# Up-projections of three feed-forward parts as three fp32r products

## What is computed

```python
def swiglu(h, w1, w3, w2):
    return (jax.nn.silu(h @ w1) * (h @ w3)) @ w2
...
def conv_ffn(h, w_up, conv_w, conv_b, w_down):
    val, gate = jnp.split(h @ w_up, 2, axis=-1)
    gate = lax.conv_general_dilated(gate, conv_w.astype(gate.dtype), window_strides=(1,),
...
    return (jax.nn.silu(gate) * val) @ w_down
```

## Time and profile before

| | before |
|---|---|
| median of three runs | 2951.45 us (2946.42 to 2951.50) |
| the profiled execution | 2939.45 us |
| its span in the trace | 2937.4 us |
| TensorE busy | 2642.8 us (90%) |
| VectorE busy | 963.7 us (33%) |
| ScalarE busy | 580.1 us (20%) |
| TensorE's mean granted clock | 0.963 of 2.4 GHz |

### The profile page before, as it was taken

One profiled execution on the slowest core, in us unless ns is written; L12 is line 12 of the kernel. 1 busy time (PEld: TensorE's weight loads), 2 busy tenths in 40 slices (PEclk: granted clock), 3 DMA queues, 4 the chain that ended last, 5 costly groups with the idle time before them and its releaser, 6 DMA issues.

```text
span 2937.4 us, 37122 instructions
## 1 busy us (share of the span) xinstructions
PE 2642.8 (90%) x15307; PEld 1697.0 (58%) x15307; DVE 963.7 (33%) x1571; ACT 580.1 (20%) x913; POOL 213.0 (7%) x256
## 2 busy tenths in 40 slices
PE   5998999999778878879999999989989998788998
PEld 2764758744433434436767767765447855554883
DVE  2304420011401001005646656640123115992111
ACT  2111610001100000004545535510001111001110
POOL 1401200000000000000000000000000032550000
PEclk8998999999899999999999999989999999888999
DMA  8527164456899999998757747754537444504441
GB/s 298 101 100 242 23 206 150 153 187 259 335 395 392 395 395 393 394 394 295 258 169 264 258 172 254 248 184 145 205 133 233 157 153 149 229 1 149 146 157 57
DMA packets 287695, 648.51 MB, mean 221 GB/s; under 512 B 12498, under 2 KB 102765, under 8 KB 274176
## 3 DMA queue, kind: packets, MB, share of 16 engines
q10 hardware_dynamic: 151440, 358.68, 33.5%
q1 hardware_dynamic: 129744, 272.83, 26.6%
q0 software_dynamic: 6368, 14.96, 2.5%
HBM read 645.38 MB, written 1.05 MB: 220 GB/s over the span
## 4 chain that ended last, share of the span: by engine, by line
PE 71%; DMA 13%; DVE 7%; ACTq 4%; issue 3%; ACT 1%; POOL 0%; DVEq 0%; POOLq 0%
PE bank L1368 21%; PE bank L1384 12%; DMA ring<-in_moe_w 11%; PE bank L591 5%; PE bank L593 4%; PE bank L592 4%; PE bank L1635 4%; ACTq L459 3%; PE bank L606 3%; DVE H L1996 2%; PE bank L603 1%; PE bank L1723 1%; DVE arena L1203 1%; PE bank L565 1%; PE bank L1526 1%
## 5 line engine op out<-in xcount | busy, mean ns | idle before, releaser
L1368 PE MATMUL bank<-HT,ring 128*128 128x256 f32 x2816 | 616.4, 382 | 5.4 <-issue 2.7
L1368 PEld LDWEIGHTS bank<-HT,ring 128*128 128x128 f32 x2816 | 538.8, 192 | 83.4 <-issue 4.6
L944 DVE TENSOR_TENSOR w_low<-ring,w_high 128x1024 fp32r<-128x1024 f32 x252 | 305.3, 1224 | 127.9 <-ACT w_high L749 125.7
L1384 PE MATMUL bank<-ring,arena 128*128 128x512 f32 x784 | 340.7, 596 | 0.7 <-ACT arena L1104 0.7
L749 ACT ACTIVATE w_high<-ring 128x1024 fp32r<-128x1024 f32 x252 | 265.3, 1059 | 195.6 <-PE bank L593 194.0
L1384 PEld LDWEIGHTS bank<-ring,arena 128*128 128x128 f32 x784 | 149.6, 191 | 188.8 <-issue 187.5
L565 PE MATMUL bank<-ring,arena 128*64 128x256 f32 x1120 | 135.8, 385 | 43.7 <-DMA ring<-in_moe_w 43.6
L526 PE MATMUL bank<-ring,arena 128*64 128x256 f32 x1120 | 134.9, 384 | 44.2 <-DMA ring<-in_moe_w 44.2
L928 DVE TENSOR_TENSOR HT<-HT,bank 128x256 f32<-128x256 f32 x35 | 14.7, 421 | 442.7 <-PE bank L565 425.6
L591 PE MATMUL bank<-w_high,tokens_low 128*128 128x512 f32 x336 | 144.3, 429 | 11.3 <-DVE w_low L944 8.5
L551 PE MATMUL bank<-ring,arena 128*64 128x512 f32 x560 | 132.3, 601 | 21.8 <-DMA ring<-in_moe_w 21.8
(11 more groups left out here) (368 smaller groups left out, 2810.6 us busy)
## 6 DMA issues: line engine op xcount, KB each, us to landing
ring<-in_moe_w ACTq DMA_DIRECT2D x340, 1024.0 KB, 13.9
ring<-in_w_ada SPq DMA_DIRECT2D x48, 1024.0 KB, 7.9
ring<-in_ada_w SPq DMA_DIRECT2D x48, 1024.0 KB, 5.0
ring<-in_ffn_w_up SPq DMA_DIRECT2D x44, 1024.0 KB, 5.0
ring<-in_ffn_w SPq DMA_DIRECT2D x33, 1024.0 KB, 5.2
ring<-in_ret_w_in SPq DMA_DIRECT2D x24, 1024.0 KB, 5.1
ring<-in_ffn_w_down SPq DMA_DIRECT2D x22, 1024.0 KB, 4.8
ring<-in_w_in SPq DMA_DIRECT2D x12, 1024.0 KB, 11.4
```

The lines of the kernel that those rows point to most:

```text
L944: dve.tensor_tensor(out=WL[half % SPLIT][:, :], in0=slot(i)[:, HALF * (half % 2):HALF * (half % 2) + HALF], in1=WH[half % SPLIT][:, :], op ...
L1368: mm = pe.matmul(PS[b][:, SEQ * m:SEQ * m + SEQ], w[:, k, P * m:P * m + P], src[:, k, :], start=k == 0, stop=k == KD - 1)
L1384: mm = pe.matmul(bank(4 + 2 * t + n), lhs(2 * j + k)[:, P * t:P * t + P], w[:, k, BANK * n:BANK * n + BANK], start=j + k == 0, stop=j == t ...
```

## The change

In pairs 1 to 10 of each of the three parts, an up-projection is formed as three fp32r products instead of one fp32 product: low tokens x high weights, high x high, and high tokens x low weights. Pair 0 stays as it was. Once per part ScalarE copies `HT` to `HT_HIGH` and VectorE subtracts it into `HT_LOW` (over `H`). Each tile is split in halves of 1024 numbers per partition: ScalarE copies a half to one of eight buffers `UP_HIGH` in the arena, and VectorE writes half minus high back into the same place of the ring (`RING_LOW` is a second name for the ring). Both engines split pair j+1 in their iteration j, ahead of what they do for pair j.

```diff
+            def split_columns(i, n, b):
+                for m in range(2):
+                    o, c = PS[b][:, SEQ * m:SEQ * m + SEQ], slice(P * m, P * m + P)
+                    for k in range(KD):
+                        high, low = UP_HIGH[(n + k // 4) % 8][:, k % 4, c], low_of(i)[:, k, c]
+                        pe.matmul(o, high, HT_LOW[:, k, :], start=k == 0, stop=False)
+                        pe.matmul(o, high, HT_HIGH[:, k, :], start=False, stop=False)
+                        mm = pe.matmul(o, low, HT_HIGH[:, k, :], start=False, stop=k == KD - 1)
+                return mm
...
-                        st.need(pe, i)
-                        columns(st, i, 2 * (j % 2) + s, HT).then_inc(st.done, 1)
+                        if j == 0:
+                            st.need(pe, i)
+                            columns(st, i, s, HT).then_inc(st.done, 1)
+                        else:
+                            pe.wait_ge(sem("ht_low"), 2 * UP[up] + 2)
+                            pe.wait_ge(sem("up_low"), UP_HALVES * UP[up] + 4 * (j - 1) + 2 * s + 2)
+                            split_columns(i, 4 * (j - 1) + 2 * s, 2 * (j % 2) + s).then_inc(st.done, 1)
...
+                    if j + 1 < FF // 256:
+                        for n, tile, k in split_halves(j + 1):
+                            if k == 0:
+                                st.need(act, base + tile)
+                                if n >= 8:
+                                    st.wait_done(act, base + tile - 4)
+                            act.activation(UP_HIGH[n % 8][:, :, :], cols_of(base + tile, KD)[:, k:k + 4, :], ACT.Copy).then_inc(sem("up_high"), 1)
...
+                        for h in range(2):
+                            k = slice(4 * h, 4 * h + 4)
+                            dve.wait_ge(sem("ht_high"), 2 * UP[up] + h + 1)
+                            dve.tensor_tensor(out=HT_LOW[:, k, :], in0=HT[:, k, :], in1=HT_HIGH[:, k, :], op=ALU.subtract).then_inc(sem("ht_low"), 1)
+                    if j + 1 < FF // 256:
+                        for n, tile, k in split_halves(j + 1):
+                            dve.wait_ge(sem("up_high"), UP_HALVES * UP[up] + n + 1)
+                            dve.tensor_tensor(out=low_of(base + tile)[:, k:k + 4, :], in0=cols_of(base + tile, KD)[:, k:k + 4, :],
+                                              in1=UP_HIGH[n % 8][:, :, :], op=ALU.subtract).then_inc(sem("up_low"), 1)
```

More of the change, by code:

```diff
@@ L200, in build @@
         ring = sb("ring", [P, RING, TILE])
+        ring_at = nc.sbuf_base - 4 * RING * TILE
         X = sb("X", [P, TT, D])
+        h_at = nc.sbuf_base
         H = sb("H", [P, TT, D])
@@ L413, in build, with low_of, split_halves @@
         EID_R = in_ad(720 + 2 * TT * NEXT, COLS)
+        UP = {"ffn_up": 0, "cf_up0": 1, "cf_up1": 2}
+        TURN_OF = {"ffn_up": "ffn", "cf_up0": "cf0", "cf_up1": "cf1"}
+        UP_HALVES = 4 * (FF // 256 - 1)
+        UP_HIGH = [parts(f"up_high{i}", arena_at, 14336 + HALF * i, 4, SEQ) for i in range(8)]
+        RING_LOW = parts("ring_low", ring_at, 0, RING, TILE)
+        HT_HIGH = parts("ht_high", arena_at, 8192, KD, SEQ)
+        HT_LOW = parts("ht_low", h_at, 0, KD, SEQ)
+        def low_of(i):
+            return RING_LOW[:, i % RING, :].rearrange("p (k n) -> p k n", k=KD)
+        def split_halves(j):
+            return [(2 * (j - 1) * 2 + h, 2 * j + h // 2, 4 * (h % 2)) for h in range(4)]
         NT = len(moe_tiles)
@@ L1806, in gated_ffn @@
                     b = 2 * (j % 2)
+                    if j == 0:
+                        for side in ("ht_act", "ht_dve"):
+                            act.wait_ge(sem(side), 2 * (TURN[TURN_OF[up]] + 1))
+                        for h in range(2):
+                            act.activation(HT_HIGH[:, 4 * h:4 * h + 4, :], HT[:, 4 * h:4 * h + 4, :], ACT.Copy).then_inc(sem("ht_high"), 1)
+                    if j + 1 < FF // 256:
[5 more added lines that the diff above has]
+                            act.activation(UP_HIGH[n % 8][:, :, :], cols_of(base + tile, KD)[:, k:k + 4, :], ACT.Copy).then_inc(sem("up_high"), 1)
                     if j == 2 and spread:
@@ L2084, in gated_ffn @@
                     b = 2 * (j % 2)
+                    if j == 0:
+                        for side in ("ht_act", "ht_dve"):
+                            dve.wait_ge(sem(side), 2 * (TURN[TURN_OF[up]] + 1))
+                        for h in range(2):
+                            k = slice(4 * h, 4 * h + 4)
[6 more added lines that the diff above has]
+                                              in1=UP_HIGH[n % 8][:, :, :], op=ALU.subtract).then_inc(sem("up_low"), 1)
                     if j == 0 and spread:
```

## The result

The changed kernel takes 2874.56 us (median of four runs, 2870.81 to 2877.83) against 2949.89 us before, a ratio of 0.9746 (95% interval 0.9729 to 0.9763), 75 us less. The forecast was 2888 us, its range 2852 to 2940. Further down each ratio is taken against runs of the kernel before made beside the kernel in question (median 2946.16 us for all but the last experiment, 2943.68 us for that one).

The account below looks back on a forecast made before the run. TensorE alone was taken to bound the up-projections: 415.1 us of calls removed, 351.4 us of new products added, 63.7 us saved, splitting and transfers costing nothing. With runs 12 us above the profiled execution, 2888 us; range 2852 to 2940.

Parts of the forecast that it names:

- What bounds the parts: Up-projections: TensorE busy all of it, nothing else sets the time; shorter products shorten the span if feeding keeps up.
- The pace p: Time per new 256-column fp32r product with its own 128 x 128 weight load: 122 ns, middle of 117 and 127.
- its two rows: L493's fp32 products at 114.7 ns spoke for 117; wide rounds' 512-column fp32r products at 233.3 ns for 127.
- The range of 112 to 131: Pace in ns with nothing else on the path: savings 92 to 38 us, 2859 to 2913 us, chance 78%.
- The floor that the prediction read from L493: 128-column fp32 products with full loads stand 114.7 ns apart, so p below 110 ns is hard to expect.
- The sum: TensorE: 960 calls removed, 415.1 us, against 2880 new products at 122 ns, 351.4 us; 63.7 us saved.
- The split's cover: ScalarE and VectorE split pair j+1 during pair j; low parts stand 5.6 us in, 6 us early, costing nothing.
- the forecast 4 us: Start of first part: fourth tile's low part done at 430.1, TensorE asks at 434.1; cover 4 us, cost zero.
- Loads not hidden: Up-projections: load can't run under the product ahead, p 217 ns, 3161 us, slower; chance 7%.
- A shared path: Up-projections: loaded weights and streamed columns share one path, p about 140 ns, saving 11.9 us, 2940 us; chance 6%.
- its 640 columns: Shared-path count for wide-round products: 233.3 ns are 640 columns, loaded and streamed, so 384 make 140 ns.
- The split as the bound: Each pair held up by ScalarE copy, VectorE subtraction, TensorE; at 1 us a pair 30 us, 2918 us; chance 6%.

Follow-up runs that it names:

- the last experiment: First two fp32r products of a chunk exchanged (high x high first), against the change with first and third down-projections split too: 2838.84 us, 0.9643 of before.
- The split beside the old products: Against the change: halves split and waited for, but every pair formed as old fp32 products, low part written over the high one: 0.9987 of before.
- the 128-token run: Against the change: each product streams 128 tokens instead of 256, with the full weight load: 111.8 ns a product, first part 122.41 us; whole time not comparable.
- the kernel with the products alone: Against the change: only pair 1's split left, its buffers reused for pairs 2 to 10: first part 128.39 us, 118.0 ns a product; whole time not comparable.

## Why the prediction was right, point by point

**What bounds the parts.** TensorE alone, as read from the earlier trace rows. The split beside the old products shows it from one side (all new work, no new time), the shorter products from the other. This mechanism carried the forecast, and it held.

**The pace p.** Forecast 122 ns, measured 121.3. The value lies between its two rows, but neither row's reason is right. The overhead over the columns at the full clock is 14.6 ns at 256 columns and 20 at 512, and it changes with the number of weight columns, with where the third product's weights come from or repeat, and with the order of the products. The range of 112 to 131 was well founded; that the middle came within 1 ns is luck, since the same three products in another order take 118. The floor that the prediction read from L493 is real, at 112 ns.

**The sum.** 2880 x 121.3 = 349.3 us stand for 415.1, 65.8 us less; the forecast had 63.7. The three lengths give 67.1; the 1.3 us more are in the third part, whose start ran longer at the lower clock level before (granted clock of the whole stretch 0.98, now 0.99). That is no gift of the change: the same 64 instructions of pair 0 there took from 15.5 to 17.1 us in the profiles of the experiments.

**What is not in it.** The medians differ by 75 us, with 70 to 80 from the interval, the parts by 67. The kernel with the split beside the old products was itself 0.13% (0.02 to 0.25%), 4 us, faster than before without any shorter stretch. And the same first 400 us end at 414.8 to 427.1 us in these profiles, although no instruction in them was changed. So single profiles wander by several us outside the parts: from before to after, what stands ahead of the first part became 5.4 us shorter, the stages between the first and the second 5.3 us longer, those between the second and the third 2.1 us shorter. No stage grew by what a part gave up, but the some 8 us that the medians have beyond the parts belong to no step of the change that I could show. Of the 13 us by which the forecast was too high, these are the largest piece; 3.4 us are the parts (67.1 against 63.7), and 1.6 us the median of before, 2951.45 then and 2949.89 with a fourth run.

**The split's cover.** Forecast: low parts stand 5.6 us into a pair. In the profile VectorE's four subtractions for pair 3 end at 445.86 us, 5.4 us after TensorE was done with pair 1 at 440.47. VectorE has 57.5, 78.7 and 76.7 us in the three parts, where 60 to 80 in each were forecast; the first lies just under. The start of the first part passed without a wait of TensorE. The cover there was larger than the forecast 4 us, because the prediction set the low part of the fourth tile against the moment at which TensorE asks for the third: in the profile the third tile's low part is done at 423.25 us and asked for at 428.5, the fourth's at 426.24 and 434.5.

**The rivals.** Loads not hidden (p near 217): excluded by the timeline of the change, a load begins with the product ahead of it, on the whole array. The Trainium skill, page "TensorE: Matmul & The Clock Gate", section "The mechanism", under "What overlaps and what doesn't", ties that overlap to another row group. This trace contradicts it: 2875 of the 2880 loads begin within 8 ns of the start of the product ahead, all on the whole array. A shared path (p near 140): excluded by the pace. The prediction held that nothing in the trace spoke against it, but the fp32 instructions did: 216.2 ns at 256 columns and 429 at 512 are 0.83 ns a column with some 3 ns left over, where a load on the same path would have added 47 ns by the prediction's own count (128 of its 640 columns in 233.3 ns). The split as the bound: it takes twice VectorE's subtractions to get there, and then it costs 9.1 and 3.9 us in the two convolution parts and nothing in the first.

The formula of the Trainium skill (page "TensorE: Matmul & The Clock Gate", section "Back-to-back issue gap"), N/2.4 + 2.5 ns, makes 109 ns of 256 columns, an estimate that was 12 ns short. With fp32r the measured distance was above it in each form tried; at 128 tokens, where it would give 56 ns, the load's floor of 112 ns stands in its place.

## What to carry to other kernels

A product of fp32 numbers that stands as two slow instructions (2 x 216 ns at 256 columns) is worth splitting into three fp32r products (3 x 121 ns) where the stage is bound by TensorE and two other engines have some 5 us to spare in each pair of 11.65; at 512 columns the ratio is better (858 to 700 ns), at 128 columns three products of 112 ns would stand against two instructions of 112 (an estimate from the 128-token run and L493), so there the load's floor takes the gain away. Before building it, read the nearest products of the same kind for the pace and the nearest ones with the same load for the floor, and let the forecast stand between them. When an experiment changes values that a router reads, compare stages and not times.

## What was not expected of the hardware

The distance of fp32r products depends on more than their shape. With the same 256 columns and full loads the three of a group stood 121, 124 and 119 ns apart in the change, 364 ns the group, and 354 ns when the first two changed places or when the third load repeated the second's weights from the arena. With 64 weight columns a product took 115.8 ns and with 32 it took 117.9, more again.

It is not the instructions alone that fix it. In the kernel with the products alone the instructions and buffers of the three parts are the same, without a wait of TensorE. Yet from the third changed pair on the three products of a group stand 122, 113 and 119 ns apart in the first part, 120, 121 and 116 in the second, and 118, 118 and 118 in the third; 96 products take 11.31, 11.41 and 11.31 us. So the distance of a single product in a group is no price to reckon with; the length of a group is a better one, and even that moved by 3 ns between the parts of this one run. No run here parts addresses from repetition, and none shows what divides the time within a group, so the cause is open.

That ScalarE and VectorE read and write the same memory all the while did not matter: in the first part 118.0 ns without them, 118.1 with them.
